# GpSimd issues the cached keys and values, SyncE the weights, in a one-layer decoder step

## The chip, the cores and the metric

The kernel runs on one core of one Trainium2 chip. The metric is the time of one execution on the device in microseconds (us). TensorE is the matmul engine (PE in the rows, PEld for its weight loads), DVE is VectorE, ACT is ScalarE, POOL is GpSimd; SPq is SyncE's instruction queue, which in this kernel only issues transfers (DMAs).

## The reference, cut to what matters

One layer of a decoder on 256 prompt tokens and 8 sequences of 4 sample tokens, all in float32, model width 2048:

```python
def run_layer(x, c, mixer, w_ada, b_ada, g_ffn1, w1_ffn1, w3_ffn1, w2_ffn1, g_mix, w_out,
              g_ffn2, w1_ffn2, w3_ffn2, w2_ffn2):
    sh1, sc1, gt1, sh2, sc2, gt2, sh3, sc3, gt3 = adaln_params(c, w_ada, b_ada)
    x = x + MACARON * gt1 * swiglu(modulate(x, g_ffn1, sh1, sc1), w1_ffn1, w3_ffn1, w2_ffn1)
    heads, state = mixer(modulate(x, g_mix, sh2, sc2))
    x = x + gt2 * (heads @ w_out)
    x = x + MACARON * gt3 * swiglu(modulate(x, g_ffn2, sh3, sc3), w1_ffn2, w3_ffn2, w2_ffn2)
    return x, state
```

The mixer projects with `w_in` (6 x 1024 columns and the forget gate), norms queries and keys per head, and attends with 8 paged "fox" heads and 8 dilated window heads. The prompt attends to itself; the samples also attend to a cache: 8 pages of 128 keys and values for each sequence and fox head (found by `page_table`), and 640 window keys and values for each dilated head. The new keys, values and log-forgets are outputs beside `y`.

## The kernel before, in words

All work is float32 in two parts: each weight tile of 1 MB (128 x 2048) lands in `raw` (two buffers), ACT rounds it to `w_hi` (`split_high`, L1087), DVE subtracts to `w_lo` (`split_low`, L1385), and PE does three matmuls for each 128 rows: hi x hi, hi x lo, lo x hi (L720 to L722, 288 columns each). `w_hi` and `w_lo` have two buffers too. PE walks segments in program order: the first FFN (to 1032 us in the trace), the projection `mix` (49 tiles, 24 pairs), a prompt-attention loop of 18 steps, `w_out`, the second FFN. Each engine's order is written out by hand; semaphores join them.

The cache is consumed inside `mix` and the steps. It is cut into 104 **halves** of 1 MB: `HALVES`, 64 of the fox pages, then 40 of the windows. A fox half is four DMAs of 256 KB (one page of each of four sequences), whose addresses are read from `pages` by `value_load`, four for every two halves. A window half is one DMA of 1 MB, or four in home E. Each half lands in one of its **homes** (A, B, C, D, later A, B, C, E, then A, B, E; in the steps W, X, Y, Z and A), and may be asked for when PE has used the half that lay there (`kv_used`). PE uses the halves at fixed points of the pairs (`WHERE`), behind tile 0 (point 1) and tile 1 (point 3) of a pair, up to three at point 1 and two at point 3, and two in each step (L909 for keys, L913 for values).

In the kernel before, SyncE issues everything of this in one order: tile t of `w_in` (`slot`, L476, waits until tile t - 2 is split), then the halves that belong behind it (`load_half`, L538 and L546). GpSimd issues side transfers: the log-forgets, and the four stores of new keys and values, 1152 KB each, from `z` (L613 and L630), as each is finished, plus `selw` and `toe` (a bias table of 1 MB, L627).

Behind each norm of the residual, PE runs the first pair of tiles on unnormed columns (`scaled_pair`), to be multiplied by the root afterwards (`scaled`), then the second pair interleaved as the normed columns appear (`second_pair`, needs `h_ready`), then the pairs in order. In the second FFN unit 0 (silu times gate) comes before unit 1, and tile pair 2 starts when both have freed their banks (`acc_a_read`). In `mix`, ACT computes the root of the head norms with two table loads (`head_root`, L1236 and L1237), and DVE refines it (`head_norm`, L1680 to L1687).

The order of the waits in `load_half`, as before:

```python
if kind == 0 and c == 0:
    for j in range(GB):
        i = (GB * g + j) * PAGES + p
        page_of[j] = sp.value_load(pages[0:1, i:i + 1], min_val=0, max_val=POOL - 1)
if before(m) is not None:
    sp.wait_ge(S["kv_used"], before(m) + 1)
```

Of the kernel before, what the change touches and what calls it, by code (L numbers as in the profile page):

```python
# [37 lines left out]
P = 128  # L38
# [13 lines left out]
WT = 5  # L52
# [29 lines left out]
PAIR_Z = (0, 2, 4, 6, 8, 10, 12, 14, 32, 34, 36, 38, 16, 18, 20, 22, 24, 26, 28, 30, 40, 42, 44, 46)  # L82
# [118 lines left out]

def last_in(*names, until=HALVES):

    return max(i for i in range(until) if HOME[i] in names)
# [25 lines left out]
def decoder_layer(nc, xT, cT, gT, bada, nwT, bfg, relb, pt, cst, cst2, ohrev, addrev, selh,  # L230
# [9 lines left out]
    with ExitStack() as ctx:  # L240
# [47 lines left out]
        u_hi = (None, h_hi, at("u_hi", [P, KT, T], F32R, mix0))  # L288
        u_lo = (None, h_lo, at("u_lo", [P, KT, T], F32R, mix0 + KT * T * 4))
        u_own = su[:, 0:2 * TS].rearrange("p (k b s) -> p k b s", k=2, s=NS)  # L290
# [22 lines left out]
        adr = at("adr", [HEADS, REV], F32, vn0 + 5632)  # L313

# [40 lines left out]
        def kv(m, j):  # L355
# [22 lines left out]
            act_chain dve_chain y_stored heads_stored v_stored ss_read ld_att ld_rel ld_selw ld_pages  # L378
# [19 lines left out]
        KIND = (dict(n=PAGES, q=0, k=8, v=32, new=C_NEW_FOX), dict(n=WT, q=16, k=24, v=40, new=C_NEW_DIL))  # L398
# [30 lines left out]
        def _(sp):  # L429
# [31 lines left out]
            def slot(seg, j, i):  # L461
# [10 lines left out]
                else:  # L472
                    b = j // 2 if j < FA_TILE else (j - 1) // 2
                    row = 0 if j == FA_TILE else 1 + PAIR_Z[b] + (j - tile_no(b, 0))
# [40 lines left out]
            def load_half(m):  # L515

                G = max(i for i in range(SIDES) if m >= FIRST_OF[i])
                kind, g = G // GROUPS, G % GROUPS
                a, n = m - FIRST_OF[G], KIND[kind]["n"]
                v, p, c = a // (2 * n), a // 2 % n, a % 2  # L520
                if kind == 0 and c == 0:
                    for j in range(GB):
                        i = (GB * g + j) * PAGES + p
                        page_of[j] = sp.value_load(pages[0:1, i:i + 1], min_val=0, max_val=POOL - 1)
                if before(m) is not None:
                    sp.wait_ge(S["kv_used"], before(m) + 1)
                elif HOME[m] in "AB":
                    sp.wait_ge(S["x_stored"], 16)
                    sp.wait_ge(S["h_ready"], H_END)
                elif HOME[m] in "CD":  # L530
                    sp.wait_ge(S["h_ready"], H_END)
                elif HOME[m] == "E":
                    sp.wait_ge(S["bias_done"], 2)
                else:
                    sp.wait_ge(S["w_used"], 2 * (mix.n0 + TILES - (1 if HOME[m] in "WX" else 0)))
                if kind and HOME[m] != "E":
                    src = (winv if v else wink)[GB * g:GB * g + GB, p, :, 512 * c:512 * c + 512]
                    sp.dma_start(whole[HOME[m]][:, :, :], src.rearrange("a p n -> p a n"))\  # L538
                      .then_inc(S[f"kv_landed{HOME[m]}"], 16)
                    return  # L540
                for j in range(GB):
                    if kind == 0:
                        src = (vpool if v else kpool)[bass.ds(page_of[j], 1), :, 512 * c:512 * c + 512]
                    else:
                        src = (winv if v else wink)[GB * g + j:GB * g + j + 1, p, :, 512 * c:512 * c + 512]
                    sp.dma_start(kv(m, j), src.rearrange("a p n -> p (a n)")).then_inc(S[f"kv_landed{HOME[m]}"], 16)  # L546
# [1466 lines left out]
```

## Time and profile before

| | us |
|---|---|
| median of 3 runs | 2530.42 (2529.33 to 2534.91) |
| the profiled execution | 2532.02 |
| its span, first to last instruction | 2530.4 |
| PE busy in the span | 2444.4 (97%) |
| DVE, ACT, POOL busy | 1190.1, 910.4, 45.1 |
| DMA: bytes and mean rate | 619.52 MB, 245 GB/s |

PE is busy nearly everywhere, so the time is PE's work and the short holes in it. A hole shows in the timeline of PE as a bracket behind a row: how long PE stood idle before that instruction, and what released it. "DMA share" of a window is the mean busy share of the 16 DMA engines (it can read slightly above 1), PEclk the granted TensorE clock as a share of 2.4 GHz. A DMA's time to landing runs from its issue to the last byte; a transfer that queues behind others in the same queue has their time in it.

### The profile page before, as it was taken

The page shows a single profiled execution, that of the slowest core. Times are in us where ns is not written, and L with a number is a line of the kernel's source. Part 1 is how long each engine was busy: PE and PEld are TensorE (multiplying, and loading weights), DVE is VectorE, ACT ScalarE, POOL GpSimd, SP SyncE. Part 2 cuts the span into 40 slices and gives each one's busy share as a digit, 9 for nine tenths or more (in the row PEclk, how much of TensorE's full clock was granted, in tenths as well). Part 3 has the DMA queues.
Part 4 walks back from the last instruction along what each step waited for, and adds up shares of the span by engine and source line. Part 5 has one row for each costly group of instructions (what it writes and reads, how often), then busy time and mean ns, then how long its engine had stood idle before and what let it go on. Part 6 is the DMA issues. An engine that isn't in the chain of part 4 may idle for free.

```text
span 2530.4 us, 57187 instructions
## 1 busy us (share of the span) xinstructions
PE 2444.4 (97%) x23159; PEld 2326.6 (92%) x23159; DVE 1190.1 (47%) x1903; ACT 910.4 (36%) x1134; POOL 45.1 (2%) x87
## 2 busy tenths in 40 slices
PE   4899999999999999999999998999999999999999
PEld 4899999999999999999788765998999999999999
DVE  2344444344444446774344434566445444454444
ACT  2332322332223334664244323455333333333332
POOL 0032000000000000000000000000000000000000
PEclk8999999999999999999999999999999999999999
DMA  8988777777887764558899998444444444454444
GB/s 326 395 318 302 284 291 289 293 276 276 300 302 285 282 235 152 211 189 316 313 330 345 360 353 323 173 164 150 166 163 157 171 165 163 158 170 166 165 166 153
DMA packets 140007, 619.52 MB, mean 245 GB/s; under 512 B 17896, under 2 KB 24320, under 8 KB 90736
## 3 DMA queue, kind: packets, MB, share of 16 engines
q1 hardware_dynamic: 135792, 608.54, 65.8%
q0 software_dynamic: 4096, 9.27, 1.0%
q8 instruction: 90, 1.47, 0.2%
q14 instruction: 29, 0.24, 0.0%
HBM read 608.29 MB, written 11.03 MB: 245 GB/s over the span
## 4 chain that ended last, share of the span: by engine, by line
PE 86%; DMA 7%; DVE 2%; SPq 2%; ACT 2%; issue 1%; DVEq 0%; ACTq 0%
PE banks L720 25%; PE banks L721 25%; PE banks L722 24%; PE banks L641 5%; DMA adax<-in_w_ada_dram 2%; DMA raw<-in_w_in_dram 2%; PE banks L909 1%; PE banks L913 1%; SPq L546 1%; DMA kv_y<-in_winv_dram 1%; PE banks L851 1%; DVE w_lo L1385 1%; DMA adaw<-in_w_ada_dram 1%; DMA kv_b<-in_wink_dram 1%; PE banks L688 0%
## 5 line engine op out<-in xcount | busy, mean ns | idle before, releaser
L720 PE MATMUL banks<-h_hi,w_hi 128*128 128x288 f32 x3664 | 1088.5, 297 | 14.1 <-DVE w_lo L1385 9.5
L721 PE MATMUL banks<-h_lo,w_hi 128*128 128x288 f32 x3664 | 1081.9, 295 | 0.0
L722 PE MATMUL banks<-h_hi,w_lo 128*128 128x288 f32 x3664 | 1080.9, 295 | 0.0
L1385 DVE TENSOR_TENSOR w_lo<-raw,w_hi 128x1024 fp32r<-128x1024 f32 (+2 forms) x670 | 764.3, 1182 | 591.0 <-ACT w_hi L1087 589.6
L1087 ACT ACTIVATE w_hi<-raw 128x1024 fp32r<-128x1024 f32 (+2 forms) x670 | 672.1, 1025 | 924.3 <-PE banks L722 521.6
L720 PEld LDWEIGHTS banks<-h_hi,w_hi 128*128 128x128 f32 x3664 | 689.9, 188 | 40.2 <-issue 31.3
L721 PEld LDWEIGHTS banks<-h_lo,w_hi 128*128 128x128 f32 x3664 | 689.9, 188 | 0.6
L722 PEld LDWEIGHTS banks<-h_hi,w_lo 128*128 128x128 f32 x3664 | 689.7, 188 | 0.0
L720 PE MATMUL banks<-g_hi,w_hi 128*128 128x288 f32 x1376 | 409.1, 297 | 0.1
L721 PE MATMUL banks<-g_lo,w_hi 128*128 128x288 f32 x1376 | 406.6, 295 | 0.0
L722 PE MATMUL banks<-g_hi,w_lo 128*128 128x288 f32 x1376 | 406.4, 295 | 0.0
L720 PEld LDWEIGHTS banks<-g_hi,w_hi 128*128 128x128 f32 x1376 | 259.4, 188 | 4.3 <-issue 3.2
L721 PEld LDWEIGHTS banks<-g_lo,w_hi 128*128 128x128 f32 x1376 | 259.5, 189 | 0.0
L722 PEld LDWEIGHTS banks<-g_hi,w_lo 128*128 128x128 f32 x1376 | 259.5, 189 | 0.0
L1194 ACT ACTIVATE su<-banks 128x288 f32<-128x288 f32 x83 | 34.1, 411 | 512.2 <-PE banks L722 510.6
L1563 DVE TENSOR_TENSOR tmps<-banks,par 128x32 f32<-128x32 f32 x112 | 21.4, 191 | 272.8 <-PE banks L722 272.8
L1580 DVE TENSOR_TENSOR gf<-su,banks 128x288 f32<-128x288 f32 x86 | 39.1, 454 | 204.8 <-PE banks L722 203.1
L641 PE MATMUL banks<-adaw,sc 128*32 128x128 f32 x3584 | 109.4, 274 | 1.8 <-DMA adaw<-in_w_ada_dram 1.8
L641 PEld LDWEIGHTS banks<-adaw,sc 128*32 128x32 f32 x3584 | 94.4, 110 | 11.1 <-issue 9.0
L641 PE MATMUL banks<-adax,sc 128*32 128x128 f32 x1024 | 38.4, 315 | 36.1 <-DMA adax<-in_w_ada_dram 35.9
L641 PEld LDWEIGHTS banks<-adax,sc 128*32 128x32 f32 x1024 | 33.5, 127 | 39.9 <-issue 24.0
L1567 DVE SCALAR_TENSOR_TENSOR x<-banks,par,x 128x256 f32 (+1 forms) x112 | 54.2, 484 | 16.1 <-DVE x L1566 15.5
(250 smaller groups left out, 1198.2 us busy)
## 6 DMA issues: line engine op xcount, KB each, us to landing
raw<-in_w_dram SPq DMA_DIRECT2D x166, 1024.0 KB, 4.8
adaw<-in_w_ada_dram SPq DMA_DIRECT2D x112, 1024.0 KB, 6.7
raw<-in_w_dram SPq DMA_DIRECT2D x64, 896.0 KB, 4.5
raw<-in_w_in_dram SPq DMA_DIRECT2D x49, 1024.0 KB, 8.0
adax<-in_w_ada_dram SPq DMA_DIRECT2D x32, 1024.0 KB, 12.7
raw<-in_w_dram SPq DMA_DIRECT2D x32, 960.0 KB, 4.7
raw<-in_w_out_dram SPq DMA_DIRECT2D x16, 1024.0 KB, 5.0
kv_a<-in_vpool_dram SPq DMA_DIRECT2D x36, 256.0 KB, 4.9
```

The source lines that it names most:

```text
L546: sp.dma_start(kv(m, j), src.rearrange("a p n -> p (a n)")).then_inc(S[f"kv_landed{HOME[m]}"], 16)
L641: last = pe.matmul(ada_part[32 * j:32 * j + 32, 0:P], sc32[:, kt, :], cols[:, :, k, :, j, :], start=kt == 0, stop=kt == KT - 1, tile_posit ...
L720: pe.matmul(bank[:, 0:T], hi, m_hi[:, k, :], start=k == 0, stop=False)
L721: pe.matmul(bank[:, 0:T], hi, m_lo[:, k, :], start=False, stop=False)
L722: last = pe.matmul(bank[:, 0:T], lo, m_hi[:, k, :], start=False, stop=k == nk - 1)
L851: return pe.transpose(dst, src, ident[0:src.shape[0], 0:src.shape[0]])
L909: last = pe.matmul(main[32 * j:32 * j + 32, p // 4, (p % 4) * P:(p % 4 + 1) * P], qbd[j // 2][:, j % 2, 32 * h:32 * h + 32], kv(m, j)[:, i ...
L1087: act.activation(w_hi[:, r, a:b], raw[:, r, a:b], ACT.Copy).then_inc(S["hi_ready"], 1)
L1194: act.activation(su[:, :], (scaled_banks[0] if scaled else acc_a)[:, 0:T], ACT.Silu).then_inc(S["acc_a_read"], 1)
L1385: dve.tensor_tensor(w_lo[:, r, a:b], raw[:, r, a:b], w_hi[:, r, a:b].bitcast(F32), ALU.subtract).then_inc(S["lo_ready"], 1)
L1567: dve.scalar_tensor_tensor(xp, bank[:, 0:TP], par[:, bass.ds(gate * NC, 1)], xp, ALU.mult, ALU.add).then_inc(S["acc_b_read" if j else "acc ...
L1580: dve.tensor_tensor(gf[:, :], su[:, :], b[:, 0:T], ALU.mult).then_inc(S["acc_b_read"], 1)
```

## The change

1. All 104 halves are issued by GpSimd, in its own queue, in one loop over `m`; SyncE keeps the weights, the saves and reloads of `x`, and `y`. The waits of each half stay. The value loads, `lf_out`, `selw` and `toe` stand in the same GpSimd order.
2. The four stores of new keys and values are issued together, after the first unit of `w_out` has left its bank, instead of during `mix` and the steps. The waits on them move from inside `w_out` to the second FFN's first silu. For this `z` is laid out with the queries first (`PAIR_Z`, `Z_PARTS`; the order of the weight tiles is unchanged), `u_lo` lies over `big` and `u_own` in `tmps`, with one more wait of DVE on itself in `part_low`.
3. Behind the norm of `mix`, ACT and DVE split tile 0 of pair 3 before the first head norm instead of after it.
4. Behind the norm of the second FFN, unit 1 (plain) comes first and unit 0 (scaled) second: pair 2 of PE waits for one bank release instead of two, tile (2, 0) is split earlier, and the multiplications of `scaled` come after unit 1.

```diff
@@ sync
-            def load_half(m):
...
-            page_of = [None] * GB
-            m = 0
             for t in range(TILES):
                 if 2 <= t < 4:
                     sp.wait_ge(S["shift_sum"], t - 1)
                 slot(mix, t, 0)
                 if t == 2:
                     sp.wait_ge(S["acc_b_read"], mix.rb)
                     sp.dma_start(x_dram, x[:, :, :]).then_inc(S["x_stored"], 16)
-                    sp.wait_ge(S["ld_pages"], 16)
-                if 4 <= t < 8:
-                    load_half(m)
-                    m += 1
...
-            for m in range(m, FIRST_OF[3] + 2 * WT):
-                load_half(m)
             slot(out, 0, 0)
             slot(out, 1, 0)
-            for m in range(FIRST_OF[3] + 2 * WT, HALVES):
-                load_half(m)
@@ gpsimd
-            store_heads(0, 8)
-            pool.wait_ge(S["acc_b_read"], done(11))
-            store_heads(2, 32)
...
+            for m in range(HALVES):
+                if m < 4:
+                    pool.wait_ge(S["lo_ready"], 2 * (mix.n0 + 3 + m))
+                if m == 4:
+                    pool.wait_ge(S["lf_ready"], 1)
+                    pool.dma_start(lf_out, lf[:, :]).then_inc(S["heads_stored"], 16)
+                if m == HOME.index("E"):
+                    pool.wait_ge(S["bias_done"], 2)
+                    pool.dma_start(selw[:, :], selh).then_inc(S["ld_selw"], 16)
+                if m == TOE_AT:
+                    pool.wait_ge(S["kv_used"], last_in("B") + 1)
+                    pool.dma_start(toe[:, :, :], ...)
+                load_half(m)
             pool.wait_ge(S["head_ready"], 2 * HEADS)
+            pool.wait_ge(S["acc_a_read"], out.ra + 1)
+            for n, z0 in enumerate((16, 24, 32, 40)):
+                store_heads(n, z0)
@@ tensor
+                third = seg.norm is not None and isinstance(i, int) and i == 2
-                pe.wait_ge(S["acc_a_read"], 1 if early else seg.ra + i)
+                pe.wait_ge(S["acc_a_read"], 1 if early else seg.ra + (1 if third else i))
@@ scalar
+            def scaled_first(seg):
+
+                split_high(seg, 0, 2)
+                act.wait_ge(S["heads_stored"], 5 * 16)
+                unit_silu(seg, 1, acc_a, 0)
+                split_high(seg, 1, 2)
+                act.wait_ge(S["pair_scaled"], 1)
+                unit_silu(seg, 0, scaled_banks[0], 1)
+                unit_silu(seg, 2, acc_a, 2)
...
-                        if r == 2:
-                            act.wait_ge(S["heads_stored"], 4 * 16)
-                            act.wait_ge(S["v_stored"], 16)
...
                 if b == 2:
                     head_squares(0)
-                    split_high(mix, tile_no(b, 1), 0)
+                    split_high(mix, tile_no(2, 1), 0)
+                    split_high(mix, tile_no(3, 0), 0)
                     head_root(0)
                     head_squares(1)
                     continue
@@ vector
+                dve.wait_ge(S["u_ready"], KT // 2 * (r - 1) + 1 + i)
...
+                        split_low(seg, 0, 2)
+                        gated_unit(seg, 1, 0)
+                        split_low(seg, 1, 2)
+                        shift_read(2)
+                        for j in range(2):
+                            scaled(scaled_banks[j][:, 0:T], j).then_inc(S["pair_scaled"], 1)
+                        dve.wait_ge(S["pair_scaled"], 2)
+                        gated_unit(seg, 0, 1)
...
+                if b == 2:
+                    split_low(mix, tile_no(3, 0), 0)
+                    z_copy(2, 0)
+                    head_norm(0)
+                    continue
```

## Rows read from the trace of the kernel before

**Rows 1.** The page: PE's busy time. Then the window of the cache region.
```profile
PE 2444.4 (97%) x23159; PEld 2326.6 (92%) x23159; DVE 1190.1 (47%) x1903; ACT 910.4 (36%) x1134; POOL 45.1 (2%) x87
...
1150.00:1591.00 441.00, 414.29 (x4386) 332.19 (x4384) 184.31 (x353) 161.18 (x274) 3.66 (x6) 0.98 0.91 334
```
Columns of a window: its bounds and length, busy us (instructions) of PE, PEld, DVE, ACT and POOL, PEclk, DMA share, GB/s.

**Rows 2.** Timeline of PE: start, duration, instruction, idle before it and its releaser.
```profile
1215.20 0.37 PE L720 MATMUL banks<-h_hi,w_hi 128*128 128x288 f32 x1 [1.92 <-DVE w_lo L1385]
1223.99 1.93 PE L851 MATMUL banks<-cs,ps 128*128 128x128 f32 x9 [2.21 <-ACT ps L1260]
1297.53 0.46 PE L882 MATMUL banks<-big,lfr 128*128 128x128 f32 x2 [1.55 <-DVE after L1731]
1375.92 1.06 PE L913 MATMUL banks<-kv_a,pst 128*32 128x512 f32 x8 [2.95 <-ACT pst L1268]
```

**Rows 3.** Timeline of SyncE's queue, then of ACT, 1211 to 1223 us.
```profile
1211.32 13.02 SPq L476 DMA_DIRECT2D raw<-in_w_in_dram  x3
...
1220.54 2.00 ACT L1087 ACTIVATE w_hi<-raw 128x1024 fp32r<-128x1024 f32 x2 [5.79 <-DMA raw<-in_w_in_dram]
1222.45 1.09 ACT L1257 ACTIVATE ps<-banks,nm 128x1024 f32<-128x1024 f32 x1
```

**Rows 4.** The two other late tiles: timelines of DVE, SyncE's queue and ACT.
```profile
1287.86 2.36 DVE L1385 TENSOR_TENSOR w_lo<-raw,w_hi 128x1024 fp32r<-128x1024 f32 x2 [7.83 <-ACT w_hi L1087]
...
1364.66 0.93 SPq L476 DMA_DIRECT2D raw<-in_w_in_dram  x2
...
1372.76 2.00 ACT L1087 ACTIVATE w_hi<-raw 128x1024 fp32r<-128x1024 f32 x2 [5.91 <-DMA raw<-in_w_in_dram]
```

**Rows 5.** Windows: a crowded stretch of the cache region, and w_out.
```profile
1330.00:1370.00 40.00, 37.92 (x560) 35.78 (x559) 20.36 (x28) 18.68 (x22) 0.00 (x0) 1.00 1.03 394
1591.50:1700.00 108.50, 108.46 (x864) 107.81 (x864) 71.89 (x141) 48.67 (x63) 0.00 (x0) 1.00 0.50 177
```

**Rows 6.** Windows of 3.5 us with a lowered clock.
```profile
1223.80:1227.30 3.50, 3.31 (x16) 3.25 (x17) 2.92 (x4) 3.26 (x7) 0.00 (x0) 0.57 0.62 201
1729.40:1732.90 3.50, 3.48 (x14) 3.48 (x15) 3.23 (x5) 1.55 (x2) 0.00 (x0) 0.51 0.36 75
```

**Rows 7.** Timeline of PE: first, longest and last of 13 waits for halves.
```profile
1252.14 1.07 PE L913 MATMUL banks<-kv_c,pst 128*32 128x512 f32 x8 [0.37 <-DMA kv_c<-in_vpool_dram]
1469.47 0.75 PE L909 MATMUL banks<-kv_a,qbd 128*32 128x128 f32 x20 [1.83 <-DMA kv_a<-in_wink_dram]
1583.54 1.06 PE L913 MATMUL banks<-kv_y,pst 128*32 128x512 f32 x8 [0.75 <-DMA kv_y<-in_winv_dram]
```

**Rows 8.** GpSimd's DMAs: two rows of its timeline, one of the page's issues.
```profile
125.07 1.99 POOL L600 DMA_DIRECT2D rbr<-in_relb_dram  x4
...
134.04 0.53 POOL L604 DMA_DIRECT2D lfc<-in_lfpool_dram  x1 [0.97 <-issue]
...
out_kv_out_dram<-z POOLq DMA_DIRECT2D x4, 1152.0 KB, 8.9
```

**Rows 9.** SyncE issues a fox half; PE uses the first and the 64th.
```profile
1160.93 1.94 SPq L546 DMA_DIRECT2D kv_a<-in_kpool_dram  x4
...
1141.37 1.08 PE L909 MATMUL banks<-kv_a,qbd 128*32 128x128 f32 x32
...
1434.07 1.04 PE L913 MATMUL banks<-kv_b,pst 128*32 128x512 f32 x8
```

**Rows 10.** Behind the norm of mix: two waits of PE, one of ACT.
```profile
1074.51 0.37 PE L720 MATMUL banks<-h_hi,w_hi 128*128 128x288 f32 x1 [1.17 <-DVE w_lo L1385]
1083.90 0.37 PE L720 MATMUL banks<-h_hi,w_hi 128*128 128x288 f32 x1 [1.85 <-DVE w_lo L1385]
...
1082.34 1.28 ACT L1236 ACT_TABLE_LOAD   x1 [1.76 <-DVE z L1687]
```

**Rows 11.** Behind the norm of the second FFN: PE's wait, ACT's table load.
```profile
1729.42 0.59 PE L720 MATMUL banks<-h_hi,w_hi 128*128 128x288 f32 x1 [3.30 <-DVE w_lo L1385]
...
1723.53 1.28 ACT L1194 ACT_TABLE_LOAD   x1 [2.67 <-DVE banks L1471]
```

More of the change, by code:

```diff
@@ L199, in before, with toe_at @@
     return max((i for i in range(m) if HOME[i] == HOME[m]), default=None)
+def toe_at():
+    return next(m for m in range(HALVES) if before(m) is not None and before(m) > max(i for i in range(HALVES) if HOME[i] == "B"))
+TOE_AT = toe_at()
 def last_in(*names, until=HALVES):
@@ L473, in slot @@
                     b = j // 2 if j < FA_TILE else (j - 1) // 2
-                    row = 0 if j == FA_TILE else 1 + PAIR_Z[b] + (j - tile_no(b, 0))
+                    a = PAIR_Z[b] + (j - tile_no(b, 0))
+                    part = a // HEADS
+                    row = 0 if j == FA_TILE else 1 + HEADS * (Z_PARTS[part] if part < 4 else part) + a % HEADS
                     ap = src[row:row + 1, :, :]
@@ L513, in _ @@
             stream(ffn1[1:])
-            def load_half(m):
[L517 to L546, printed above, removed]
-            page_of = [None] * GB
-            m = 0
             for t in range(TILES):
@@ L830, in segments @@
                         second_pair(seg, seg.norm)
-                        run(seg, pe, lambda i, seg=seg: pair(seg, i), 2)
+                        pair(seg, 2)
+                        run(seg, pe, lambda i, seg=seg: pair(seg, i), 3)
                     else:
@@ L1179, in body @@
             def body(seg, i):
-                behind = (seg.norm is not None and i in (0, 1) or (seg is out or seg is segs[1]) and i == 0) \
-                    if isinstance(i, int) else False
+                behind = (seg is out or seg is segs[1]) and isinstance(i, int) and i == 0
                 if not behind:
@@ L1202, in segments @@
                 for seg in some:
-                    peel = 2 if seg.norm is not None else 1 if seg.squares or seg is segs[1] else 0
-                    for i in range(peel):
-                        body(seg, i)
+                    peel = 3 if seg.norm is not None else 1 if seg.squares or seg is segs[1] else 0
+                    if seg.norm is not None:
+                        scaled_first(seg)
+                    elif peel:
+                        body(seg, 0)
                     if seg.squares:
@@ L1595, in body @@
             def body(seg, i, late, group=None):
-                behind = (seg.norm is not None and i in (0, 1) or (seg is out or seg is segs[1]) and i == 0) \
-                    if isinstance(i, int) else False
+                behind = (seg is out or seg is segs[1]) and isinstance(i, int) and i == 0
                 if not behind:
@@ L1628, in segments @@
                         half_gate(8, GROUPS_ADA)
-                    body(seg, 0, late)
+                    if seg.norm is None:
+                        body(seg, 0, late)
                     if seg.ada:
@@ L1781, in _ @@
                     split_low(mix, FA_TILE, 0)
-                if b > 2:
+                if b > 3:
                     split_low(mix, tile_no(b, 0), 0)
@@ L1868, in _ @@
             modulate(2)
-            shift_read(2)
-            for j in range(2):
-                scaled(scaled_banks[j][:, 0:T], j).then_inc(S["pair_scaled"], 1)
-            dve.wait_ge(S["pair_scaled"], 2)
+            dve.wait_ge(S["heads_stored"], 5 * 16)
             segments(segs[segs.index(out) + 1:])
```

101 lines of the change are left out of this document (58 added, 43 removed).

## The prediction

> **What bounds the kernel now.** First the page: PE is busy 97% of the span [rows 1], so the time is PE's work plus its holes. The work is not touched, so I read the holes. The window of the cache region, 1150 to 1591 us, has 414.3 us of PE in 441: 26.7 us of idle, more than anywhere but the start. The DMA engines there have a share of 0.91 at 334 GB/s, while crowded stretches reach 1.03 and 394 GB/s [rows 5]: the transfers are nearly a second bound, but not one through the whole region. Then the timeline of PE, hole by hole, and for each the releaser's own wait.
>
> Four holes end with an engine that waited for a weight tile. At 1215.2 (1.92 us) and 1224.0 (2.21 us) [rows 2] the tile was issued at 1211.32, behind two halves, and reached ACT 9.2 us later; the exponential that PE needs stood behind it on ACT [rows 3]. At 1297.5 (1.55 us) DVE had waited 7.83 us for a tile, and at 1375.9 (2.95 us) ACT had waited 5.91 us for one issued at 1364.66, again behind halves [rows 4]. Thirteen holes, 10.8 us together, end with a half that landed late, of which three stand in [rows 7]. Behind the norm of mix stand 1.17 and 1.85 us [rows 10], behind the second norm 3.30 us [rows 11]. The steps near 1550 to 1565 have holes of ACT's and DVE's latency, which nothing here changes. Twice the clock falls after such idleness, from 2.4 to 1.2 GHz for about 3.5 us [rows 6]: the mean over the window is 0.57 and 0.51.
>
> **The change part by part.** The sum is made against the profiled span, 2530.4 us, with 1.6 us around it (2532.0); the median of the three runs is 1.6 us lower again.
>
> *Weights on their own in SyncE's queue.* A tile may be asked for as soon as the tile two before it is split. With no half before it, it comes one pair (over 13 us) ahead, and even at half the DMA rate 1 MB takes 5.3 us (2 x 1.05 MB over 394 GB/s). So the four holes go: 1.92 + 2.21 + 1.55 + 2.95 = 8.6 us. What is late next: the exponential follows DVE's maximum at once, and PE has 48 matmuls, over 6 us, to run before it asks, so nothing of it stays. The clock's fall at 1223.8 hangs on the first two: 3.5 x (1 - 0.57) = 1.5 us. Together 10.1 us; bounds 6 (the third hole stays, since DVE has a head norm there, and the clock falls all the same) and 11.
>
> *Halves on GpSimd: the issue.* GpSimd makes 308 DMAs here, 256 of them for the fox halves. Back to back a DMA costs it 0.50 us, in its own loop with one value load 1.51 us (0.97 of gap and 0.53) [rows 8]. No row shows the mixture, so bounds: eight DMAs for two halves cost between 8 x 0.50 = 4.0 and 8 x 1.51 = 12.1 us, so 2.0 to 6.0 us a half. The code has four value loads for eight DMAs, so I take 4 x 1.51 + 4 x 0.53 = 8.2, or 4.1 us a half. PE asks for 60 halves (the first four are early) between 1141.4 and 1434.1 us [rows 9]: 292.7 us with some 13 us of holes, 4.66 us a half without them. GpSimd is thus 88% busy and not the bound, though in a pair with five halves it falls a little behind and lives on the four homes. Queued behind each of its waits are only later halves; `selw`, `toe` and `lf_out` are wanted much later.
>
> *Halves: the landing.* SyncE issues four DMAs in 1.94 us [rows 9], GpSimd in some 2.8 (0.7 each, between 0.50 and 1.51), so a half starts 0.9 us later after its home is free, and it shares the engines with a weight tile that now runs beside it. Against that, no half waits for a tile's turn, and the stores leave the region: 4 x 1.18 MB over 394 GB/s is 12 us of all engines, one of them beside the hole at 1445 and one beside that at 1514. Of the 10.8 us I leave 8.0 standing: 2.8 saved. Bounds: all gone (10.8 saved); or every one longer by 0.9 us and as many new ones of 0.9 (23 more lost).
>
> *The stores during w_out.* 4.7 MB in a window with a DMA share of 0.50 at 177 GB/s over 108.5 us [rows 5]: they fit more than four times. A weight tile needs 1 MB per 6.4 us there and has two buffers of lead. Cost 0 to 1 us, taken as 0. A store lands in 8.9 us [rows 8], so the waits now placed before the silu, 120 us later, never bind; and the waits taken out of w_out had been met. DVE's added wait on itself costs 16 times under 0.2 us on an engine busy under half the time: 0. The move of `z` costs nothing.
>
> *The order behind the norm of mix.* Both holes, 3.0 us, come from tiles split late, one behind halves in SyncE's queue, one behind the first head root on ACT. With the change PE does not wait for either, and reaches pair 3's second tile 3.8 us earlier by starts. But that tile's split stands behind the second head root, which needs DVE's first head norm; that chain (table load at 1082.34 after a wait for DVE [rows 10]) starts only 0.7 us earlier. A new hole of about 2.0 us opens there: 1.8 us saved. Bounds 0 and 3.8.
>
> *The order behind the second norm.* PE idles 3.30 us because silus 0 and 1 and the split stand between [rows 11]. Now the split is done early, but silu 1 can start only when PE has finished pair 1, and its table load (1.28 us) stands behind that wait in program order: 0.2 + 1.28 + 0.41 + 0.1 = 2.0 us of hole. 1.3 us saved, and 3.5 x 0.49 = 1.7 us more if the clock then stays up, as it did after holes of 1.92 and 2.95 us: 3.0. Bounds 0 and 5.0.
>
> **The sum.** 10.1 + 2.8 + 0 + 1.8 + 3.0 = 17.7, against 2532.0 this is 2514.3, and by the median's 1.6 us less about 2512.7; say 2512.5 us.
>
> The Trainium skill says in DMA: Bandwidth & Descriptors, section Issuing engines are not separate DMA queues, that transfers of all engines run on the same 16 DMA engines, and that issuing from several "will only save the time on the sequencer". By that, only the last two parts would be left, which is the second rival; rows 3 and 4 rather show a tile held by order, which that sentence does not speak of.
>
> **The rivals.** *Halves land late more often.* GpSimd's slower issue and the weights beside them cost 0.9 us at some ten more points (with three homes, A, B and E, a reload has two tiles' half, some 8.5 us by PE's rows, before PE asks): the sum shrinks by 9 to about 9, 2521.5 us. For it: the three-home stretch is where the longest waits are. Against: the stores are gone from there.
>
> *The second queue gives nothing*, because a late tile is late by the engines' load and not by its place, or the halves don't really run apart. Then 4.8 us from the norms are left: 2525.6 us. Against it: at 1211 to 1221 the tile stood behind two halves' issue, and the window 1222 to 1240 then ran empty.
>
> *All waits for halves go, and no new hole behind the first norm*: 8.0 + 2.0 more, 2502.5 us.
>
> *GpSimd's issue is the bound (slower than before).* Place: the fox halves. If a half costs h, the region takes 60 x h instead of 292.7 us, and it decides from h = 4.66, where the gain of the region starts to be lost, and makes the kernel slower in all from 4.96. At h = 5.2, inside the bounds of 2.0 to 6.0, it is 312 us: +19.3 and -4.8 from the norms, 2545 us; at 6.0 it is 2593. For it: 88% busy by my own count. Against: the 64 DMAs of the loop show 0.53 us throughout although DVE worked beside them.
>
> The Trainium skill gives a mechanism for this: SBUF — State Buffer, section SBUF: two separate sides, says that while DVE runs a float32 copy from SBUF to SBUF, GpSimd cannot write the descriptors of its DMAs and they starve. DVE has few such copies here, most of its work being subtractions and PSUM reads; so the trace of before speaks for little of it, and no run shows it yet.
>
> **How the numbers follow.** Forecast 0.47; halves late more often 0.17; all waits gone 0.12; queue gives nothing 0.08; GpSimd bound 0.16. What a measurement of this kernel can tell from no change is about 0.2%, 5.1 us: so faster 0.47 + 0.17 + 0.12 = 0.76, same 0.08, slower 0.16. The range reaches from just under the best case, 2500, to 2534, which takes in the second queue that gives nothing and most of the larger costs of the halves, and leaves out the bound on GpSimd and a little more.
>
> **What would show it.** In the profile after: ACT's waits for `raw` of w_in in the waits view fall to a small part and no hole has a split as its releaser between 1200 and 1400 us. GpSimd shows 308 DMAs in the region and four starts of one fox half lie 2.8 us apart at most; if it has rows without any wait between them from 1230 us on and PE waits for halves, the issue is the bound. PE's waits for halves sum to about 8 us. Behind the first norm the hole is before pair 3's second tile. Behind the second norm PE's hole is 2.0 us with the table load in it, and PEclk stays at 1. In w_out PE stays whole beside the stores. The prediction is wrong if a DMA of GpSimd takes over 0.9 us, or if halves land over 6 us after their last issue.

## The result, and the profile after

The changed kernel is slower. Its median is 2551.53 us (2550.44 to 2553.49, 4 runs) against 2531.91 us (2529.33 to 2534.91) of the kernel before on the same chip: a ratio of 1.0074, 95% interval 1.0061 to 1.0087, some 19 us. The forecast was 2512.5 us.

The page of the profiled execution, lines of the span, PE and POOL as in [rows 1], then the queues:

```profile
span 2550.9 us, 57167 instructions
...
PE 2457.5 (96%) x23159; PEld 2337.1 (92%) x23159; DVE 1191.4 (47%) x1903; ACT 912.5 (36%) x1134; POOL 218.1 (9%) x395
...
q1 hardware_dynamic: 77616, 499.47, 53.4%
q0 software_dynamic: 35648, 118.34, 12.9%
```

PE executes the same 23159 matmuls in both kernels, in the same order. So each can be paired with itself in the other trace, and the delay, its start after less its start before, is a step curve: flat where nothing happens, with a step at each hole that came or went. Summed between fixed matmuls it gives this table (us). "Late-tile stretches" are the three around 1215, 1297 and 1376 us of [rows 2]; the cache region runs from the 11420th to the 16130th matmul, 1113 to 1592 us before.

| stretch | before | after | difference | forecast |
|---|---|---|---|---|
| start, to 254 us | 241.6 | 244.0 | +2.4 | 0 |
| end of the first FFN | 93.3 | 96.4 | +3.1 | 0 (DVE's wait) |
| norm of mix | 59.0 | 62.0 | +2.9 | -1.8 |
| cache region, late-tile stretches | 36.4 | 25.6 | -10.8 | -10.1 |
| cache region, the rest | 442.9 | 465.1 | +22.3 | -2.8 |
| w_out, first pairs | 35.7 | 40.0 | +4.3 | 0 |
| second norm | 11.7 | 8.2 | -3.6 | -3.0 |
| all else | | | 0.1 | 0 |
| PE's last matmul | 2526.3 | 2547.0 | +20.8 | -17.7 |

The first row is chance: nothing of the code there is changed, the hole is one late transfer of `w_ada` (2.61 us at 251.75), and in the twelve kernels below, with the same code in that place, the stretch takes 239.6 to 245.8 us.

Two steps went as forecast. The tiles no longer come late: in the waits view of ACT, 1100 to 1450 us, its waits for `raw` were 165.3 us before and are

```profile
ACT w_hi L1088 <- DMA raw<-in_w_in_dram: 7.9, 2, 4.4
```

(total, times, longest), and no hole of [rows 2] is left. Behind the second norm PE's hole is 1.28 us, where [rows 11] has 3.30 and the forecast 2.0: the table load started 0.5 us before PE stopped and not behind it. Timeline of PE, then of ACT:

```profile
1751.73 0.40 PE L719 MATMUL banks<-h_hi,w_hi 128*128 128x288 f32 x1 [1.28 <-ACT su L1194]
```
```profile
1749.97 1.28 ACT L1194 ACT_TABLE_LOAD   x1
1751.27 0.41 ACT L1194 ACTIVATE su<-banks 128x288 f32<-128x288 f32 x1
```

The loss is in PE's waits for halves. From the waits view of PE, 1100 to 1620 us, the four largest:

```profile
PE banks L910 <- DMA kv_e<-in_wink_dram: 4.4, 2, 2.5
PE banks L914 <- DMA kv_a<-in_vpool_dram: 4.3, 2, 2.8
PE banks L910 <- DMA kv_e<-in_kpool_dram: 3.4, 1, 3.4
PE banks L914 <- DMA kv_y<-in_winv_dram: 3.1, 1, 3.1
```

All such rows sum to 23.0 us, before to 10.7 (the longest of [rows 7] was 1.83). Counted from start to start of the matmuls, as from here on, it is 24.6 us in 14 waits against 11.6 in 13. The rest of the 22.3 us is mostly the clock: it falls to 1.2 GHz at three of these waits (at 1360.8, 1449.6 and 1483.7 us), for 6.8 us each, and at a fourth (1599.8 us) for 10.2 us, where the kernel before had 3.4. Between 1449.84 and 1456.27 that alone delays PE by 3.0 us, and by 2.4 us between 1601 and 1606.5. Window of one:

```profile
1449.60:1456.40 6.80, 6.80 (x31) 5.58 (x24) 0.00 (x0) 1.11 (x1) 1.33 (x3) 0.50 1.02 398
```

How a half's time is made up can be followed by its semaphores. From both traces, means over the 60 fox halves from the fifth on (us; the one that comes first into home E has no release and is left out where that counts): from the release of its home by PE to its first issue, from the first to the last issue of its four DMAs, last issue to landing, and all together; "start" is the time from release to first issue of a half that finds its issuer already waiting.

```
            start   to issue   issuing   landing   together
before      0.16      1.64       1.71      6.17       9.52
after       0.63      2.06       1.87      7.56      11.47
```

### The profile page after: what moved, and what is told of

Its sections match the earlier page's. It is cut to its first block, busy times and chain, and to the rows that moved or that the text cites. A ratio compares the mean times of both kernels' runs of the same rounds, so it can differ in the third digit from the quotient of the medians.

```text
span 2550.9 us, 57167 instructions
## 1 busy us (share of the span) xinstructions
PE 2457.5 (96%) x23159; PEld 2337.1 (92%) x23159; DVE 1191.4 (47%) x1903; ACT 912.5 (36%) x1134; POOL 218.1 (9%) x395
## 3 DMA queue, kind: packets, MB, share of 16 engines
q8 instruction: 91, 1.49, 0.2%
## 4 chain that ended last, share of the span: by engine, by line
PE 87%; DMA 6%; DVE 3%; issue 2%; ACT 1%; SPq 0%; POOL 0%; POOLq 0%; DVEq 0%; ACTq 0%
PE banks L719 25%; PE banks L720 25%; PE banks L721 24%; PE banks L640 5%; DMA adax<-in_w_ada_dram 2%; PE banks L910 1%; PE banks L914 1%; DVE w_lo L1395 1%; PE banks L852 1%; DMA adaw<-in_w_ada_dram 1%; PE banks L848 1%; DMA raw<-in_w_out_dram 0%; PE banks L687 0%; DMA kv_y<-in_winv_dram 0%; PE banks L1025 0%
## 5 line engine op out<-in xcount | busy, mean ns | idle before, releaser
L719 PEld LDWEIGHTS banks<-h_hi,w_hi 128*128 128x128 f32 x3664 | 692.8, 189 | 36.3 <-issue 25.9
L1690 DVE COPY z<-banks 128x288 f32<-128x288 f32 x46 | 21.0, 456 | 177.4 <-PE banks L721 177.3
L608 POOL DMA_DIRECT2D kv_a<-in_kpool_dram x32 | 17.2, 538 | 883.2 <-DVE h_lo L1446 838.9
```

Of the source, the lines that this page charges most:

```text
L719: pe.matmul(bank[:, 0:T], hi, m_hi[:, k, :], start=k == 0, stop=False)
```

## The experiments

Times are medians, each beside runs of the kernel before on the same chip; the ratios are the figures to compare. The medians of before were 2533.09, 2531.76 and 2532.47 us in the three groups of four. Given beside them are the waits for halves and the "rest" of the cache region, the row above of 442.9 and 465.1 us. Accounts A and B are the theories A and B of the expectation. The stretches come from one trace of each kernel, so here is how well they repeat: where the cache region's code is the same, the rest is 442.9 and 442.7 us (as before), 438.9 and 439.1 (one queue), 447.7 and 446.1 (exchanged), 465.1, 465.2, 468.4 and 473.7 (as in the changed kernel), and the late-tile stretches with one queue are 33.0 and 37.8.

**One queue again.** All halves go back to SyncE, the rest of the change stays.

```diff
+            for t in range(TILES):
+                slot(mix, t, 0)
...
+                while (BIAS_AT[1] if before(m) is None else WHERE[before(m)]) <= spot and HOME[m] not in "WXYZ":
+                    load_half(m)
+                    m += 1
```

> The changed kernel with all halves back in SyncE's queue, in the order of the kernel before. The stores during w_out, both orders behind the norms and DVE's wait on itself stay. By the delays of PE's instructions from one trace to the other, the second queue gains 10.5 us (late tiles and the clock's fall behind them) and loses 22 us (halves). If that account holds, this kernel takes 11.5 us less than the changed one, 2540 us, 8 us over the kernel before; PE's waits for halves are back at some 11 us and the late tiles at 1215 to 1376 us are back. The rival, that the loss lies in the other parts and the halves are only its victims (later start, shifted beside other work), has it at 2550 us with waits for halves of over 20 us.

Measured: 2535.39 us, ratio 1.0011 (1.0000 to 1.0023). Waits for halves 8.3 us, rest of the region 438.9 us. The queue made the loss, the first account, and more than its 11.5 us, some 16 by the ratios: without the stores beside them, the halves wait less than in the kernel before, and of the three late-tile stretches the first takes 14.1 us instead of 18.5. The other two are back.

**Smaller packets of weights.**

```diff
+                if seg is mix:
+                    c = KT * P // 4
+                    for q in range(4):
+                        sp.dma_start(raw[:, r, c * q:c * q + c], ap[:, :, c * q:c * q + c]...)
```

> The changed kernel, but SyncE asks for each tile of w_in in four DMAs of 512 columns, so that a packet of a weight carries 2 KB and not 8 KB. Theory A, the two queues are served packet by packet, and a tile's 8 KB packets (some 330 ns) against a half's 4 KB (137 ns) leave the half under a third of the engines while a tile is in flight: now a half gets over half of them, lands sooner (mean 7.6 us after its last issue in the changed kernel, expected about 6.7), PE's waits for halves fall from 23 us to 10 to 16, the time to about 2543 us. Theory B, the halves are late because GpSimd issues slower and its queue is slower by itself: landing stays at 7.6 us, waits at 23 us, the time at 2551 us or a little more, since SyncE's tiles take longer.

Measured: 2557.14 us, ratio 1.0097 (1.0079 to 1.0115); landing 7.7 us, waits 25.4 us. The numbers are those of account B: account A's gain did not come. The sharing that A rests on is real all the same: while a tile is in flight the two queues send about a packet each in turn. Queues in the changed kernel, 1209.5 to 1212 us (packets, MB, share of 16 engines), and with small packets, 1211 to 1217 us:

```profile
q1 hardware_dynamic: 79, 0.65, 67.1%
q0 software_dynamic: 99, 0.32, 34.6%
```
```profile
q0 software_dynamic: 444, 1.45, 63.3%
q1 hardware_dynamic: 474, 0.87, 40.7%
```

Of the 99 packets, 20 are of four bytes: that leaves 79 of 4 KB against 79 of 8 KB. (In the median of the region a packet of 4 KB takes 159 ns, not the 137 of the expectation, and one of 8 KB 309.) With 8 KB against 4 KB the tile takes two thirds of the engines, with 2 KB two fifths. But then it is in flight for longer. The eleventh half, early in the region, lands sooner (5.1 us after its last issue, 7.1 in the changed kernel), the mean of all does not. My reading, which no run separates from the three more issues a tile: where tile and halves together fill the engines, the bytes put in front of a half count and not the size of their packets. The Trainium skill, DMA: Bandwidth & Descriptors, section Queues, rings and completion order, says that each engine takes its queues in turn, a packet at a time. The packet counts in the changed kernel agree with it; those with small packets, 426 of the tile's 2 KB beside 355 of 4 KB, do so roughly.

**Tiles held back.** SyncE waits, before each tile, until the halves that stood ahead of it in the kernel before have landed.

```diff
+                        sp.wait_ge(S[f"kv_landed{HOME[m]}"], n)
+                        m += 1
                 slot(mix, t, 0)
```

> The changed kernel, both queues kept, but SyncE asks for a tile of w_in only when the halves that stood ahead of it in the kernel before have landed. Theory A, a tile that is asked for a pair ahead takes its megabyte of the engines from the halves that PE wants first: now the halves of the fox heads land within 6.3 us of their last issue on average (7.6 in the changed kernel, 6.2 in the kernel before), PE's waits for halves fall from 24.6 us to 12 to 16 us, late tiles come back for some 5 us, and the time is 2542 to 2548 us. Theory B, the halves are late because GpSimd's queue is slow in itself: landing stays above 7.3 us, the waits stay above 22 us, and with the late tiles on top the time is 2555 us or more.

Measured: 2588.29 us, ratio 1.0228 (1.0212 to 1.0245). For the halves it went as account A said: landing 6.6 us, waits 13.0 us. Its time was far off, since tiles are late by much more than the 5 us I allowed. From the waits view of PE, 1100 to 1660 us:

```profile
PE banks L727 <- DVE w_lo L1403: 30.5, 12, 4.3
```

So a tile that runs beside the halves does delay them (7.6 against 6.6 us of landing), and a tile that waits for their landing is worse: PE then waits for tiles, and the clock stands at 1.2 GHz for 65 us of the region instead of 37.

**Queues exchanged.** Halves alone on SyncE, tiles of `w_in` on GpSimd.

```diff
@@ gpsimd
+            for t in range(8, TILES):
+                slot(mix, t, 0, pool)
@@ sync
+            for m in range(4, FIRST_OF[3] + 2 * WT):
+                load_half(m)
```

> The changed kernel with the queues exchanged: SyncE asks for the halves and nothing else, GpSimd for the tiles of w_in from the ninth on, one DMA each. A half is again issued by the faster engine and its queue, but a tile still comes as early as its buffer allows and runs beside the halves. Theory A (tiles beside the halves): landing stays at 7.2 to 7.7 us after the last issue, PE's waits for halves at 18 us or more of 24.6 (the start comes 0.6 us earlier, which 12 waits feel), time 2543 to 2551 us. Theory B (GpSimd's issue and queue): landing 6.2 us, waits 11 us or less, and no late tile, so 2538 us or less.

Measured: 2535.98 us, ratio 1.0025 (1.0014 to 1.0035); landing 7.2 us, waits 13.3 us, rest of the region 447.7 us, all three late-tile stretches as short as in the changed kernel (25.6 us). The truth lies between the accounts, and this run divides the loss. From one queue to two with the faster engine for the halves, the rest of the region grows by 8.8 us (438.9 to 447.7), which the late tiles give back (33.0 to 25.6 us). From there to the changed kernel it grows by 17.4 us more, and what differs is that the two streams change engines: the halves come from GpSimd, in packets of 4 KB instead of 2, and the tiles from SyncE. By kinds of halves (waits in us):

```
             fox halves   window halves in mix   in the steps
before          4.3              4.7                 2.6
one queue       4.5              2.8                 1.1
exchanged      11.7              0.4                 1.2
changed        14.4              6.0                 4.1
held back       4.6              4.2                 4.2
```

**A later start, by itself.** The exchanged queues with one more value load between a half's wait and its first DMA.

```diff
+                sp.value_load(pages[0:1, 0:1], min_val=0, max_val=POOL - 1)
                 if kind and HOME[m] != "E":
```

> The kernel with exchanged queues, but SyncE reads one more page number (0.55 us) between a half's wait for its home and its first DMA, in all 104 halves; it stands for the later start of a half on GpSimd (0.63 us after the release where SyncE needs 0.16). Theory A, each half that PE waits for passes its delay on, and delays add: PE's waits for halves go from 13.3 us to 19 to 23 us, the time from 2536 to 2542 or 2545 us. Theory B, the engines' load sets when a half lands, and half a microsecond at the start is hidden in it: waits under 15 us, time under 2538 us.

Measured: 2545.51 us, ratio 1.0053 (1.0036 to 1.0071); a half that finds SyncE waiting starts 0.73 us after its release instead of 0.16, the waits are 20.6 us, the rest of the region 454.3 us. Account A. 0.57 us of start cost 7 us of time (the intervals of the two ratios allow 2 to 12), twelve times as much, and the trace of the exchanged queues has twelve waits for halves: the delays add up and don't hide in one another. The reason that I see, and that no run tests by itself: a half that PE waits for frees the home of the next one later as well. In the traces the rest of the region grew by 6.6 us. Of the 17.4 us above, 10.8 are thus not the start, although here the window halves start 0.57 us later too and in the changed kernel 0.26. That kernel has 4.0 us more of waits than this one and 37 us at 1.2 GHz where this one has 20; what makes its halves later still, no run shows.

**The order behind the norm of mix, alone in the kernel before.**

```diff
-                split_high(mix, tile_no(b, 0), 0)
+                if b != 3:
+                    split_high(mix, tile_no(b, 0), 0)
                 if b == 2:
                     head_squares(0)
-                    split_high(mix, tile_no(b, 1), 0)
+                    split_high(mix, tile_no(2, 1), 0)
+                    split_high(mix, tile_no(3, 0), 0)
```

> The kernel before with the order behind the norm of mix alone: tile 0 of pair 3 is split ahead of the first head norm. In the changed kernel ACT stood for 5.2 us before a tile that had not landed, with the first head root behind it, and PE lost 2.4 us against the kernel before. Theory A, the order itself does it, since the root now waits for a transfer that it did not wait for: 2 to 5 us more than the kernel before here too. Theory B, my forecast of 1.8 us saved is right for the order, and the halves beside that tile on the second queue made the loss: 2530 us.

Measured: 2539.19 us, ratio 1.0033 (1.0021 to 1.0045), so account A, and more than its 2 to 5 us; in the traces the stretch takes 64.8 us instead of 59.0. Its timeline of ACT, then the hole of PE:

```profile
1076.68 2.01 ACT L1087 ACTIVATE w_hi<-raw 128x1024 fp32r<-128x1024 f32 x2 [4.03 <-DMA raw<-in_w_in_dram]
1078.70 1.28 ACT L1236 ACT_TABLE_LOAD   x1
1080.00 0.74 ACT L1236 ACTIVATE yh<-banks,eps 128x576 f32<-128x576 f32 x1
1080.76 1.28 ACT L1237 ACT_TABLE_LOAD   x1
1082.05 0.68 ACT L1237 ACTIVATE yh<-yh 128x576 f32<-128x576 f32 x1
```
```profile
1083.67 1.30 PE L847 MATMUL banks<-hsq,cs 128*128 128x288 f32 x2 [3.98 <-DVE th L1682]
```

ACT waits 4.03 us (5.18 in the changed kernel) for a tile before it may begin the root, and that chain of four instructions and DVE's part behind it end in PE's hole. It holds in all the traces: with the old order the stretch takes 57 to 61 us in five kernels, with the new one 62 to 66 in nine.

**DVE's wait on itself taken away.** `u_own` gets a place of its own.

```diff
-        u_own = tmps[:, :, :, :]
+        u_own = at("u_own", [P, 2, NB, NS], F32, lfr0)[:, :, :, :]
...
-                dve.wait_ge(S["u_ready"], KT // 2 * (r - 1) + 1 + i)
```

> The changed kernel without DVE's wait on itself at the end of part_low; the small tile u_own has a place of its own instead of tmps, which needs no such wait. Theory A, the wait costs 0.5 us in front of the next split of a weight, and six times in the first FFN and once at its end PE is just waiting for that split: 3.7 us less, 2548 us, the holes of 0.4 us at 967, 979, 991, 1003, 1014 and 1027 us are gone. Theory B, those small holes come from the run or from another place of u_lo: they stay, 2551.5 us.

Measured: 2551.79 us, ratio 1.0077 (1.0060 to 1.0094). In the trace account A is right: all six holes are gone and the end of the first FFN takes 93.3 us again, in this kernel and in all later ones without the wait. In the time nothing can be seen of it, so these 3 us are shown by the traces alone: the region's rest took 468.4 us here, 3.3 more than in the changed kernel, and the runs spread from 2543.6 to 2557.7. How the wait costs, in the changed kernel, timeline of DVE and of PE:

```profile
965.09 0.88 DVE L1433 SCALAR_TENSOR_TENSOR h_lo<-x,par,h_hi  x2
966.39 2.10 DVE L1395 TENSOR_TENSOR w_lo<-raw,w_hi 128x1024 fp32r<-128x1024 f32 x2 [0.42 <-DVE h_lo L1433]
```
```profile
967.67 0.40 PE L719 MATMUL banks<-g_hi,w_hi 128*128 128x288 f32 x1 [0.43 <-DVE w_lo L1395]
```

and in the kernel before, timeline of DVE:

```profile
962.70 0.88 DVE L1423 SCALAR_TENSOR_TENSOR h_lo<-x,par,h_hi  x2
963.50 2.08 DVE L1385 TENSOR_TENSOR w_lo<-raw,w_hi 128x1024 fp32r<-128x1024 f32 x2
```

The split starts 0.80 us after the instruction ahead of it without the wait, and 1.30 with it: 0.5 us, and PE stands at exactly this split.

**Stores one by one.**

```diff
-            pool.wait_ge(S["acc_a_read"], out.ra + 1)
             for n, z0 in enumerate((16, 24, 32, 40)):
+                pool.wait_ge(S["acc_a_read"], out.ra + 1 + n)
```

> The changed kernel with the four stores of new keys and values not issued together but one behind each of the first four pairs of w_out, some 13 us apart. Theory A, four stores of 1.18 MB at once take the engines for 6 us and then every second packet, so two weight tiles of w_out land late: the hole of 2.8 us at 1637 us and the clock's fall behind it go, 4.3 us less, 2547 us. Theory B, any store beside the weights makes its tile late: four smaller holes of 0.7 us or more in their place, 2549 to 2552 us.

Measured: 2551.78 us, ratio 1.0075 (1.0060 to 1.0090). Again the trace shows account A, w_out's first pairs take 35.7 us as before the change, and the time shows nothing, since the region took 8.6 us more in the profiled run, with 1.9 us more of waits for halves and 51 us at 1.2 GHz in place of 37. In the changed kernel, timelines of POOL and ACT:

```profile
1622.84 2.15 POOL L575 DMA_DIRECT2D out_kv_out_dram<-z  x4 [32.59 <-DVE x L1579]
```
```profile
1637.18 2.00 ACT L1088 ACTIVATE w_hi<-raw 128x1024 fp32r<-128x1024 f32 x2 [9.26 <-DMA raw<-in_w_out_dram]
```

Four stores at once are 4.7 MB in front of and beside the next tiles: from 1632 to 1635 us GpSimd's queue sent 71 packets and SyncE's 72. PE has its hole of 2.52 us at 1639.55.

**What was left as gain, together.** One queue, the stores one by one, the order behind the second norm; not the order behind the norm of mix, and not DVE's wait.

> What the account by stretches leaves as gains, together: one queue for halves and tiles, the stores out of the cache region but one behind each of the first four pairs of w_out, the order behind the second norm, no wait of DVE on itself (u_own in a place of its own); the order behind the norm of mix as in the kernel before. The kernel with one queue ended 1.3 us under the kernel before in the traces; with 3.6 us of DVE's waits, 2.8 us of stores together and 4.7 us at the norm of mix taken away from that it would be some 12 us faster, a ratio of 0.995. Theory B, the gains are eaten at the next wait (a half or a tile that comes too late anyway): within 0.2% of the kernel before.

Measured: 2525.08 us, ratio 0.9973 (0.9960 to 0.9985). A gain, of half the size expected: the late-tile stretches took 37.8 us in its trace, where the kernel with one queue had 33.0.

**The second queue by itself**, added to that kernel.

> The same kernel as the faster one (stores one by one, order behind the second norm, no wait of DVE on itself, order behind the norm of mix as before), with one thing changed: GpSimd asks for the halves. This is the second queue by itself. Theory A, the parts add up: the second queue costs by itself what it cost in the changed kernel against the kernel with one queue, 15 us or so, so 2538 to 2543 us, a ratio of 1.003 to 1.005. Theory B, the halves were late only since everything around them had been moved: within 0.1% of the faster kernel, 2527 us.

Measured: 2542.65 us, ratio 1.0042 (1.0027 to 1.0057), account A: 17.5 us by the ratios. The rest of the region takes 465.2 us, as in the changed kernel (465.1), and the waits are 25.3 us. The parts of the change add up, and this one is the loss.

**Exchanged queues in that kernel.**

> The faster kernel with exchanged queues: SyncE asks for the halves, GpSimd for the tiles of w_in from the ninth on. By the stages of the traces, the kernel with exchanged queues less 3.1 us of DVE's waits, 3.7 us at the norm of mix and 4.3 us of the stores is 2525 us, a ratio of 0.9975, the same as the faster kernel with one queue: what the late tiles give back is lost on halves. If separate queues were a gain in themselves as soon as the halves have the fast one, it would be under 2520 us.

Measured: 2524.99 us, ratio 0.9984 (0.9972 to 0.9997), as worked out: no better than one queue, and the runs don't tell the two apart.

**The tile ahead of halves that can wait.**

```diff
-                while (BIAS_AT[1] if before(m) is None else WHERE[before(m)]) <= spot and HOME[m] not in "WXYZ":
+                while HOME[m] not in "WXYZ":
+                    late = 2 if m in (16, 17, 18, 19, 34, 35, 50, 51) else 0
+                    if (BIAS_AT[1] if before(m) is None else WHERE[before(m)]) > spot - late:
+                        break
```

> The faster kernel, one queue, but eight of the 104 halves, which PE wants only two pairs or more later (before the pairs that take the new keys), are asked for behind the next tile of w_in and no longer ahead of it. Theory A, the tiles that come late at 1215, 1297 and 1375 us do so by their place in the queue: these three stretches take 9.3, 12.5 and 3.9 us as with two queues, where the faster kernel took 14.6, 13.7 and 9.5, and the time falls by 6 to 11 us, to about 2517 us, a ratio of 0.994. Theory B, they are late by the engines' load: the stretches stay, or the halves behind the tile are late instead, 2525 us.

Measured: 2518.52 us, ratio 0.9951 (0.9936 to 0.9966). Account A, its time a little short of the 6 to 11 us (5.6 under the faster kernel by the ratios, whose intervals just overlap): the late-tile stretches take 25.9 us, the rest 441.8 us with 10.1 us of waits. The tile that came at 1364.66 behind two halves [rows 4] now comes between two pairs of them; timeline of SyncE's queue, then of ACT, which finds it there:

```profile
1352.22 1.88 SPq L559 DMA_DIRECT2D kv_b<-in_vpool_dram  x4
1354.14 0.43 SPq L489 DMA_DIRECT2D raw<-in_w_in_dram  x1
1356.95 2.73 SPq L559 DMA_DIRECT2D kv_c<-in_vpool_dram  x4
```
```profile
1364.16 2.00 ACT L1101 ACTIVATE w_hi<-raw 128x1024 fp32r<-128x1024 f32 x2
1366.06 0.57 ACT L1288 ACTIVATE pst<-banks 128x512 f32<-128x512 f32 x1
```

Beside the same runs of the kernel before, the exchanged queues have 0.9984 (0.9972 to 0.9997): this kernel is faster than those, and than the kernel before.

## Why the prediction was wrong, point by point

*Weights on their own.* Right: 10.1 us forecast, 10.8 found, with the clock's fall at 1223.8 gone too. But a second queue was not needed for it; moving eight halves in one queue gave the same stretches.

*Halves on GpSimd, the issue.* Right that it is not the bound. A DMA comes every 0.585 us and a value load takes 0.55, so 3.4 us a half where I took 4.1, against a demand of 4.66. The rival that made the issue the bound came near in time (2545 us at 5.2 us a half) and is wrong as a cause: GpSimd still waits for PE to free a home, as between the second and the third half here. Timeline of POOL in the changed kernel:

```profile
1205.48 2.29 POOL L608 DMA_DIRECT2D kv_a<-in_vpool_dram  x4 [3.50 <-PE banks L910]
1207.83 2.29 POOL L608 DMA_DIRECT2D kv_b<-in_vpool_dram  x4
1213.91 2.29 POOL L608 DMA_DIRECT2D kv_c<-in_vpool_dram  x4 [3.80 <-PE banks L910]
```

*Halves, the landing.* This step failed, and with it the forecast. The term was 2.8 us saved and is 22.3 us lost. Three things were wrong in it.

First the size: I put the start of a half 0.9 us later and took the landing itself as unchanged; release to landing grew by 1.95 us, of which 1.4 is landing, since the tile that no longer queues behind the halves runs beside them (held back, landing was 6.6 us instead of 7.6). I had written down that a tile runs beside them and gave it no price.

Second the count: I let the absence of the stores and of a tile's turn pay for the later start. The stores were worth 4.0 us (442.9 to 438.9 with one queue), not the whole.

Third, and most, how the delays add up: in the middle of my forecast the later start cost nothing in the end, and in the first rival its own 0.9 us at ten points. But 0.57 us of start cost 7 us, and to the clock's falls behind the waits I gave no price here, though I had priced one elsewhere. My own bound of 23 us lost, every wait longer by 0.9 us and as many new, came near the 22.3 by luck: the waits grew by 13.0 us in all, from 13 to only 14 of them, and the other 9.3 us are mostly the clock. I gave that bound no weight in the middle and almost none in the range.

What the term is made of, the runs show in part: 8.8 us from one queue to the exchanged ones, 6.6 us by a later start, and 10.8 us open. That makes 26.2 us over the kernel with one queue; over the kernel before it is 22.3, since the stores gave 4.0 back. Of the 38.5 us between my sum (17.7 saved) and the traces (20.8 lost), this term has 25.1. The signs I named for it did show: the four starts of a fox half lie 1.87 us apart, well inside the 2.8 I allowed, but halves landed 7.6 us after their last issue. As a sign the 6 us were badly chosen: the kernel before already has 6.17.

*The Trainium skill's rule*, in DMA: Bandwidth & Descriptors, section Issuing engines are not separate DMA queues, would have left only the two orders, 2525.6 us. Its first half holds in these runs: two queues gave no bandwidth (321 GB/s from 1140 to 1450 us, 332 before), and no form with separate queues is faster than its like with one. Its second half, that only sequencer time is saved, says too little here: the order of the bytes changed, in both directions. The rule on GpSimd starved by DVE's float32 copies, SBUF — State Buffer, section SBUF: two separate sides, is hardly put to the test: of the 143 us that DVE was busy from 1140 to 1450 us, under 2 were such copies. GpSimd's DMA instructions for the halves took 0.54 to 0.77 us throughout.

*Stores during w_out.* Wrong: 4.3 us for 0 to 1. I compared a window's mean load, 0.50, with the stores' bytes. But they come within 2.15 us, and 9216-byte packets then take every second turn from a tile that is wanted in 6 us. One store a pair costs nothing, as the run with stores one by one shows.

*DVE's own wait.* Wrong: 3.1 us for 0. I divided its cost by DVE's mean load, under a half, and did not look at what stands behind it: the split of the next weight, at which PE arrives in six of the sixteen places.

*The order behind the norm of mix.* Wrong, 2.9 us lost for 1.8 saved. The two holes did go, but the new one is larger than my 2.0 us and in another place: not before pair 3's second tile and for its split, but ahead of pair 3's first, at the sums for the head norm, which wait for DVE behind the first head root. Timeline of PE in the changed kernel:

```profile
1088.39 2.26 PE L848 MATMUL banks<-hsq,cs 128*128 128x288 f32 x4 [2.76 <-DVE th L1697]
```

I had timed the root by an early split that would find its tile there. No row of before said that it does; ACT asked for it later. And with this hole the clock falls for 6.8 us, from 1087.8 us on, which I had at nothing: it delays PE by 2.8 us, nearly the whole loss, while the old and new holes are about equal (1.17 and 1.85 us before; 2.76 and one of 0.58 after). Alone in the kernel before the order costs 5.8 us in the trace.

*The second norm.* Right: 3.0 us forecast, 3.6 found, the clock stays up. The hole is 0.7 us shorter than forecast, since the table load did not wait for PE's last matmul.

Open is why window halves in `mix` wait 6.0 us when GpSimd issues them and 0.4 when SyncE does, with the tiles beside them in both. They start 0.26 us later; with 0.57 us more on SyncE they already waited 3.8 us (1.49 and 2.32 in the trace), so the start may be a good part of it. For the last halves of the steps a cause is at hand but was not tried: `x` comes back in SyncE's queue, in the changed kernel beside the last half, in the kernel before behind it.

## What to carry to other kernels

Before a stream is given a queue of its own, ask which of the two can wait. In one queue the order of issue is the priority; in two the engines share by packets, and the stream with slack takes what the urgent one needs. And where a buffer is asked for only when the consumer frees it, price a tenth of a microsecond by all the waits in the loop, not by one: here it came back about twelve times. Price the clock's fall behind a wait as well; here it was as large as many of the waits.

A mean load says nothing of a cost of 0. For each added wait or burst, look at the one instruction behind it and at who is standing there.

## What the runs showed of the hardware

- A DMA whose address comes from a register starts 0.63 us after the release it waits for on GpSimd and 0.16 us on SyncE (0.28 and 0.02 where the address is fixed); back to back it comes every 0.585 us there and every 0.515 here. GpSimd's transfers of the same pages go in packets of 4096 bytes (159 ns in the median), SyncE's in 2048 (84 ns), at about the same rate.
- An instruction of DVE behind a wait on DVE's own last result started 0.5 us later than without the wait (1.30 us behind the start of the one ahead, 0.80 without).
- At three waits for halves, of 2.0, 2.5 and 3.4 us, PE's clock stood at 1.2 GHz for 6.8 us each, at one of 3.1 us for 10.2 us. Behind the wait of 2.0 us this cost 3.0 us, more than the wait itself. Another of 2.75 us, at 1424.0, was followed by no fall. In the kernel before the falls behind 2.21 and 3.30 us lasted some 3.4 us.
